# Gate products: high and low parts accumulated in the same PSUM columns, in place of side by side

## The reference, cut to what matters

```python
v1, i1 = lax.top_k(s1, PEER_TOPK)
v2, i2 = lax.top_k(s2, PEER_TOPK)
cand = (v1[..., :, None] + v2[..., None, :]).reshape(T, PEER_HEADS, PEER_TOPK * PEER_TOPK)
sc, ci = lax.top_k(cand, PEER_TOPK)
e1 = jnp.take_along_axis(i1, ci // PEER_TOPK, axis=-1)
e2 = jnp.take_along_axis(i2, ci % PEER_TOPK, axis=-1)
idx = e1 * PEER_NKEYS + e2
gate = jax.nn.softmax(sc, axis=-1).astype(xn.dtype)
...
    h = jax.nn.gelu(jnp.einsum('cd,chkd->chk', xc, u[ic]))
    return jnp.einsum('chk,chkd->cd', gc * h, v[ic])
```

## Time and profile before

| | |
|---|---|
| median of 3 runs | 3075.8 us (3075.11 to 3077.78) |
| the profiled execution: its own time, its span | 3076.66 us, 3074.9 us |
| busy share of the span: PE, PEld, DVE, ACT | 98%, 85%, 66%, 50% |
| mean granted TensorE clock | 0.995 of full speed |
| DMA | 615.20 MB, mean 200 GB/s |

### The profile page before, as it was taken

The page is one execution under the profiler, slowest core; times in us unless marked ns, Lnnn a source line. Parts: engine busy times, 40 slices in busy tenths (PEclk is TensorE's granted clock), DMA queues, the critical chain, the costliest instruction groups (busy, mean ns, idle before and its releaser), DMA issues.

```text
span 3074.9 us, 45142 instructions
## 1 busy us (share of the span) xinstructions
PE 3027.6 (98%) x16816; PEld 2623.8 (85%) x16816; DVE 2029.1 (66%) x2701; ACT 1538.6 (50%) x2137; POOL 12.6 (0%) x27
## 2 busy tenths in 40 slices
PE   8999999999999999999999999999999999999999
PEld 7897898888888888888888888888888888888887
DVE  4566679976888885555555555776566777777444
ACT  3454434565666664444444444544455555555333
POOL 1000000000000000000000000000000000000000
PEclk9999999999999999999999999999999999999999
DMA  8532545565566568666666666444455555555554
GB/s 267 141 114 96 180 165 185 210 219 197 191 239 226 211 227 301 245 244 240 239 239 240 240 243 242 145 152 164 151 181 181 186 190 180 191 189 183 200 192 178
DMA packets 136931, 615.20 MB, mean 200 GB/s; under 512 B 12605, under 2 KB 49678, under 8 KB 71536
## 3 DMA queue, kind: packets, MB, share of 16 engines
q1 hardware_dynamic: 126176, 583.05, 53.2%
q10 hardware_dynamic: 9328, 21.93, 2.3%
q0 software_dynamic: 1328, 8.89, 0.7%
HBM read 578.13 MB, written 36.49 MB: 200 GB/s over the span
## 4 chain that ended last, share of the span: by engine, by line
PE 81%; DVE 5%; ACT 5%; DMA 4%; issue 3%; ACTq 0%; DVEq 0%; SPq 0%
PE bank L628 80%; ACT high L2239 3%; DMA raw<-in_experts_u_t 2%; DVE low L1262 2%; DMA raw<-in_w_in_t 1%; ACT first_both L2487 1%; DVE first L1795 1%; ACT big L2495 1%; PE bank L898 0%; PE bank L718 0%; ACT big L2466 0%; ACT big L2460 0%; DMA resid<-in_x 0%; DVE big L1620 0%; DVE resid L1893 0%
## 5 line engine op out<-in xcount | busy, mean ns | idle before, releaser
L1262 DVE TENSOR_TENSOR low<-raw,high 128x1024 fp32r<-128x1024 f32 x1008 | 1225.0, 1223 | 838.9 <-ACT high L2239 834.8
L2239 ACT ACTIVATE high<-raw 128x1024 fp32r<-128x1024 f32 x1008 | 1055.4, 1057 | 1072.7 <-PE bank L628 751.3
L628 PE MATMUL bank<-act_both,high 128*128 128x512 f32 (+1 forms) x5088 | 1174.4, 359 | 16.7 <-DVE low L1262 5.8
L628 PEld LDWEIGHTS bank<-act_both,high 128*128 128x128 f32 x5088 | 879.5, 191 | 134.0 <-issue 7.8
L628 PE MATMUL bank<-act_both,low 128*128 128x256 f32 x4240 | 715.5, 283 | 0.0
L628 PEld LDWEIGHTS bank<-act_both,low 128*128 128x128 f32 x4240 | 628.2, 191 | 33.1
L628 PE MATMUL bank<-high,weighed_high 128*128 128x512 f32 x1024 | 398.4, 389 | 0.0
L628 PE MATMUL bank<-high,weighed_low 128*128 128x512 f32 x1024 | 398.3, 389 | 0.0
L628 PE MATMUL bank<-low,weighed_high 128*128 128x512 f32 x1024 | 398.3, 389 | 0.0
L628 PE MATMUL bank<-high,act_both 128*128 128x512 f32 (+1 forms) x960 | 310.1, 393 | 2.3 <-DVE act_both L1342 2.3
L628 PEld LDWEIGHTS bank<-high,weighed_low 128*128 128x128 f32 x1024 | 192.3, 188 | 39.9
(11 more groups left out here) (286 smaller groups left out, 1919.6 us busy)
## 6 DMA issues: line engine op xcount, KB each, us to landing
raw<-in_experts_u_t SPq DMA_DIRECT2D x128, 1024.0 KB, 4.9
raw<-in_experts_v_t SPq DMA_DIRECT2D x128, 1024.0 KB, 4.8
raw<-in_w_up_t SPq DMA_DIRECT2D x88, 1024.0 KB, 4.8
raw<-in_w_in_t SPq DMA_DIRECT2D x68, 1024.0 KB, 4.8
raw<-in_w_down_t SPq DMA_DIRECT2D x44, 1024.0 KB, 4.8
raw<-in_w_out_t SPq DMA_DIRECT2D x32, 1024.0 KB, 4.8
raw<-in_peer_wq_t SPq DMA_DIRECT2D x16, 1024.0 KB, 4.8
hidden_dram<-big SPq DMA_DIRECT2D x64, 256.0 KB, 3.1
```

The costliest lines, as they stand in the source:

```text
L628: return pe.matmul(out_, lhs_t, rhs, start=start, stop=stop, skip_group_check=True)
L1262: dve.tensor_tensor(low[b][:, :], raw[r][:, HALF * which:HALF * (which + 1)], as_f32(high[b][:, :]), ALU.subtract).then_inc(low_ready[b], 1)
L2239: act.activation(high[b][:, :], raw[r][:, HALF * which:HALF * (which + 1)], ACT.Copy).then_inc(high_ready[b], 1)
```

## The change

TensorE multiplies `second` with `first_high` and then, as a second product, with `first_low`, and both go into the same 128 columns of PSUM: the second accumulates. A token now has 128 columns instead of 256, four tokens fill one bank, and the banks 5 and 7 are not used in this stage. ScalarE's copy takes the finished sum and raises `gates_copied` itself. `sum_gates` and the semaphores `gates_first` are gone, and since VectorE's loop body no longer depends on the quarter, its four loops become one.

```diff
         def gate_parts(c):
-            return bank[:, 4 + 2 * c:6 + 2 * c, :].rearrange("p b (u s e) -> p s e (b u)", s=2, e=P)
+            return bank[:, 4 + 2 * c, :].rearrange("p (t e) -> p e t", e=P)
...
                 for t in range(FOUR):
-                    m = mm(bank[:, 4 + 2 * c + t // 2, 2 * P * (t % 2):2 * P * (t % 2) + 2 * P], second[:, c, t, :],
-                           first_both[:, c, t, :, :].rearrange("p s e -> p (s e)"))
+                    at = bank[:, 4 + 2 * c, P * t:P * t + P]
+                    mm(at, second[:, c, t, :], first_high[:, c, t, :], stop=False)
+                    m = mm(at, second[:, c, t, :], first_low[:, c, t, :], start=False)
                 m.then_inc(gates_done[c], 1)
...
-            def sum_gates(q, n, j):
-
-                c = j % SLOTS
-                at = gates_out[:, q % 2, :, bass.ds(4 * FOUR * n + (FOUR * j - QUARTER * q), FOUR)]
-                dve.wait_ge(gates_first[c], 2 * n + (j // 2 + 1))
-                dve.tensor_tensor(at, at, gate_parts(c)[:, 1], ALU.add).then_inc(gates_copied[c], 1)
-
-            def gate_tile(q, n, j, last=False):
+            def gate_tile(n, j, last=False):
 
                 split_tile_low("experts_u_t", n + CHOICE_QUADS, j)
                 if not last:
                     onehots(n, j + 1)
-                sum_gates(q, n, j)
 
             onehots(0, 0)
-            for q in range(T // QUARTER):
-                with dve.Fori(GATE_QUADS // 4 * q, GATE_QUADS // 4 * (q + 1) - (q == T // QUARTER - 1)) as n:
-                    for j in range(4):
-                        gate_tile(q, n, j)
+            with dve.Fori(0, GATE_QUADS - 1) as n:
+                for j in range(4):
+                    gate_tile(n, j)
             for j in range(4):
-                gate_tile(T // QUARTER - 1, GATE_QUADS - 1, j, last=j == 3)
+                gate_tile(GATE_QUADS - 1, j, last=j == 3)
...
                 act.activation(gates_out[:, q % 2, :, bass.ds(4 * FOUR * n + (FOUR * j - QUARTER * q), FOUR)],
-                               gate_parts(c)[:, 0], ACT.Copy).then_inc(gates_first[c], 1)
+                               gate_parts(c), ACT.Copy).then_inc(gates_copied[c], 1)
```

More of the change, by code:

```diff
@@ L389, in build @@
         first_high_ready = [sem(f"first_high_ready{c}") for c in range(SLOTS)]
-        gates_first = [sem(f"gates_first{c}") for c in range(SLOTS)]
         gates_done = [sem(f"gates_done{c}") for c in range(SLOTS)]
```

## The result

The changed kernel takes 3086.7 us (median of 8 runs, 3084.8 to 3091.1) against 3075.5 us before (8 runs, 3072.1 to 3078.5): 11.2 us slower, a ratio of 1.0036 with a 95% interval of 1.0026 to 1.0047. The profiled execution took 3086.50 us against 3076.66.

A forecast was written before the change was run, and what follows sets the result against it. The ACT-DVE ring bound 50 of 64 gate tiles; afterwards PE would bound all. Dropped add 0, accumulation 0, weight-load-bound products +13.6: 3076.66 + 13.6 = 3090.3, less 0.9 a median of 3089 us; range 3075 to 3096, forecast's own 3086 to 3093.

The forecast's parts named there:

- The ring between ACT and DVE: Gate stage: ACT's split, DVE's `split_low` and `first`, ACT's `first_high`; 6.37 us a tile in 50 tiles, PE's own tile 6.07.
- The price of a product of 128 columns: PE's gate products: the weight load binds, 0.116 us each, eight a tile; tile 6.52 us, stage 411.7 against 398.0, +13.6 us.
- gate part: PE's gate products of one tile, beside hidden products of 5.59 us: 0.48 us before, forecast 0.93.
- 407.3: Gate stage in us if the Trainium skill's 107 ns a load alone set the gate part at 0.86 us: +9.3.
- 413.6 at 0.120: Gate stage in us at the forecast range's upper end, 0.120 us a product with 1.5 us of stalls: +17.
- The add at nothing: DVE in the gate stage: removing 64 adds, 44 us of busy time, and their waits gains 0.
- No stall from accumulating: PE's gate products: the second accumulating behind the first in the same columns costs no stall.
- no single tile longer than 6.52: Single longer ring tiles, worst 7.25 us, stall PE by 0, or 1.5 us at most, since halves prepared in advance cover them.
- No change: Rival, chance 0.12: products under 0.098 us keep PE's tile below the ring in the gate stage; 3076 us.
- A lower rate of fp32r below 256 columns: Rival, chance 0.11: gate products run at plain float32's rate, 0.223 us; tile 7.37 us, +68, 3144 us.
- That the add delays the ring: Rival, chance 0.03: dropping DVE's add shortens the ring, and products need 0.064 us; tile 6.10 us, -13.2, 3063 us.
- What hid 15 us of the cost: Gate stage: of 28.7 us added to PE at 0.45 us a tile, 15 us fall into waits PE already had.

The follow-up runs named there:

- products side by side: Kernel before with only its 256-column gate products cut into two of 128, standing side by side; nothing accumulates and the add stays: 3087.0 us, 1.0038.
- half the weight columns: Changed kernel with 64 instead of 128 columns of weights in each gate product, moving columns still 128: 3075.9 us, 1.0003.
- the two kernels with `first` early: DVE writes `first` for the next tile ahead of the two `split_low`: in the kernel before 3061.1 us (0.9951), in the changed kernel 3087.0 us (1.0036).
- half the moving columns: Changed kernel with 64 instead of 128 moving columns in each gate product, weight loads still 128 columns: 3087.7 us, 1.0038.

## Why the prediction was right, step by step

- *What bounds the stage.* Right. The ring between ACT and DVE paced 50 tiles before: moving `first` alone took its 15 us away. After the change PE paces all tiles.
- *The price of a product of 128 columns.* The mechanism was right, the term a little too large: 0.116 us was taken, between 0.111 and 0.120, and 0.112 was measured, the rate of the earlier trace rows, where 16 moving columns show the load alone. The row at 0.120 has 256 moving columns and says nothing of a product that is bound by its load, so the middle was the wrong choice. This makes the sum 2 us too large: +13.6 forecast, +11.5 in the stage and +11.2 in the medians; 3086.7 us lies at the lower end of the forecast's own range of 3086 to 3093, the end that was reckoned from 0.111. Two slips in the sums change nothing: with a gate part of 0.86 the stage is 63 x 6.45 + 0.86 = 407.2, not 407.3, and the 413.6 at 0.120 is without the 1.5 us of stalls that its +17 holds (415.1). The gate part itself was to be 0.9 to 1.0 us and is 0.85, since 0.05 us of its loads falls on the next hidden product. The earlier trace rows did not show what it was read for: plain float32 passes 512 moving columns in (2090.05 - 2088.34) / 4 = 0.428 us a record, so 128 would take an estimated 0.107 by the columns alone, and its 0.111 can come from either:

```profile
2088.34 1.88 PE L628 MATMUL bank<-taps,big 128*128 128x512 f32 x4
2090.05 2.12 PE L628 MATMUL bank<-big 128*128 128x64 f32 x18
```

- *The add at nothing.* Right, by two kernels: without it the kernel before is no faster, and with it the cut products are no slower. DVE's busy time fell by 37 us and not by 44; 3.8 us of the rest are in the records of `split_low`, whose union grew from 1225.0 to 1228.8 us at an unchanged mean of 1.223 us, so they overlap less and no work was added.
- *No stall from accumulating, no single tile longer than 6.52.* Right: the products side by side cost the same, with a short load each product passes in 0.060 us though it accumulates, and no wait of PE is left.
- *The rivals.* No change needed a product under 0.098 us; half the weight columns made one of 0.060, and the time was that of the kernel before, as that point says. A lower rate of fp32r below 256 columns is excluded by the same 0.060. That the add delays the ring is excluded by the kernel without it. The Trainium skill, "TensorE: Matmul & The Clock Gate", section "Back-to-back issue gap", has some 81 ns for a product of 128 columns with its load. Here it is 112 ns for four-byte weights, so the measurement decides against that figure. The section on LDWEIGHTS of the same page of the Trainium skill has the columns divided by 1.2, an estimate of 107 ns, and the trace's 112 ns is near it.
- *What hid 15 us of the cost.* Right: PE got 0.42 us more work a tile, 26.9 us over the stage, and the stage grew by 11.5. The rest fell into waits. Against a kernel whose ring has been mended the same change costs all of it: the two kernels with `first` early are 409.5 - 382.7 = 26.8 us apart in the stage.

## What to carry to other kernels

Before a product is cut into narrower ones, compare the time of its moving columns with the time of its weight load: the bound is the longer of the two, and a cut that leaves the columns in sum the same still doubles the loads. A column of weights cost about twice a moving column here (128 in 0.112 us against 512 in 0.230), so 256 moving columns just covered a full load and 128 did not. An engine that is busy for 98% of the span may have waits that its busy time does not show; the distance of starts shows them, and it tells how much of an added cost they will swallow. Where two engines hand work back and forth, the order on one of them can be worth more than its busy time: one instruction a tile moved ahead gave 15 us, and 44 us of work removed gave none.

## What was not expected of the hardware

The first of eight narrow products is followed by the second after only 0.06 us, most likely since its weights come in while the wide product before it still runs (no run tests this); the products after it keep 0.112 us, and the wide products behind them take 0.05 us more in sum. With half the moving columns the gate part is shorter still (807.17 - 806.36 = 0.81 us) and the hidden part longer (5.68), the tile the same. So where loads are the bound, the edges between kinds of products move and only the sum of the loads can be read.
